# Two more gate chunks multiplied by seven in a four-layer transformer kernel, one of their joins inside the triangular solve, and a first input in longer runs

## The reference, cut to what matters

```
h = h + 0.5 * swiglu(rms_norm(h, ffn1_norm), ffn1_w_in, ffn1_w_out)
u = rms_norm(h, mix_norm)
z_s, xbc, dt, qkv, z_d, b, a, gate_s, gate_d = split(u @ w_in)
y_s = mamba2_branch(z_s, xbc, dt, ...)            # state space
y_d = deltanet_branch(qkv, z_d, b, a, ...)        # gated delta rule
merged = sigmoid(gate_s) * (y_s @ ssm_w_branch) + sigmoid(gate_d) * (y_d @ dn_w_branch)
h = h + merged @ w_out
h = h + 0.5 * swiglu(rms_norm(h, ffn2_norm), ffn2_w_in, ffn2_w_out)
```

## Time and profile before

| | |
|---|---|
| median of 3 runs (lowest, highest) | 3190.79 us (3189.23, 3192.85) |
| the profiled execution's own time | 3191.32 us |
| its span, first to last instruction | 3189.5 us |
| PE busy / DVE busy / ACT busy / POOL busy | 3175.9 / 2379.4 / 665.3 / 281.8 us |
| granted TensorE clock, mean | 0.999 |
| share of PE in the chain that ended last | 99% |

### The profile page before, as it was taken

One profiled execution on the slowest core, in us unless ns is written; L12 is line 12 of the kernel. 1 busy time (PEld: TensorE's weight loads), 2 busy tenths in 40 slices (PEclk: granted clock), 3 DMA queues, 4 the chain that ended last, 5 costly groups with the idle time before them and its releaser, 6 DMA issues.

```text
span 3189.5 us, 59761 instructions
## 1 busy us (share of the span) xinstructions
PE 3175.9 (100%) x25296; PEld 3035.7 (95%) x25296; DVE 2379.4 (75%) x4672; ACT 665.3 (21%) x1633; POOL 281.8 (9%) x329
## 2 busy tenths in 40 slices
PE   9999999999999999999999999999999999999998
PEld 8999999999999999999999999879999999889998
DVE  6657887476666578874867898877786888876885
ACT  1113433211111134332211111211211111212211
POOL 0202000001102020000011000300021000300031
PEclk9999999999999999999999999999999999999999
DMA  5444444345445444443544444344445444343453
GB/s 204 171 156 140 143 147 151 119 159 172 171 160 172 159 136 143 150 151 120 184 172 165 167 168 165 130 149 146 150 168 172 164 168 171 119 159 133 159 173 133
DMA packets 89787, 497.52 MB, mean 156 GB/s; under 512 B 25104, under 2 KB 29616, under 8 KB 30640
## 3 DMA queue, kind: packets, MB, share of 16 engines
q1 hardware_dynamic: 70752, 489.45, 44.5%
q10 hardware_dynamic: 18768, 4.25, 0.7%
HBM read 491.55 MB, written 2.11 MB: 155 GB/s over the span
## 4 chain that ended last, share of the span: by engine, by line
PE 99%; DMA 1%; DVE 0%; ACTq 0%; SPq 0%; ACT 0%; issue 0%; DVEq 0%
PE bank L358 92%; PE bank L2109 1%; PE bank L2921 0%; PE bank L2163 0%; PE bank L2865 0%; PE bank L2902 0%; PE bank L2088 0%; DMA ring<-w 0%; DMA hT<-hT_d 0%; PE bank L531 0%; PE bank L2866 0%; PE bank L2040 0%; PE bank L2110 0%; PE bank L2126 0%; PE bank L2048 0%; PE bank L2846 0%
## 5 line engine op out<-in xcount | busy, mean ns | idle before, releaser
L358 PE MATMUL bank<-arena 128*128 128x128 f32 x9480 | 1122.4, 275 | 0.0
L358 PEld LDWEIGHTS bank<-arena 128*128 128x128 f32 x9480 | 1089.9, 192 | 0.2 <-DVE arena L1087 0.2
L358 PE MATMUL bank<-arena,ring 128*128 128x128 f32 (+1 forms) x6408 | 1000.4, 309 | 2.5 <-ACT arena L891 2.1
L358 PEld LDWEIGHTS bank<-arena,ring 128*128 128x128 f32 x6408 | 907.0, 191 | 59.2 <-issue 2.9
L358 PE MATMUL bank<-xT,ring 128*128 128x128 f32 (+1 forms) x4816 | 666.4, 292 | 0.1
L358 PEld LDWEIGHTS bank<-xT,ring 128*128 128x128 f32 x4816 | 620.2, 192 | 21.8 <-issue 1.0
L1085 DVE TENSOR_TENSOR arena<-ring 128x1024 f32<-128x1024 f32 x355 | 435.4, 1226 | 104.0 <-PE bank L358 93.5
L1032 ACT ACTIVATE arena<-bank 128x128 f32<-128x128 f32 x323 | 89.0, 275 | 990.7 <-PE bank L358 985.2
L1140 DVE TENSOR_TENSOR arena<-arena,bank 128x256 f32<-128x256 f32 x323 | 136.0, 421 | 202.3 <-PE bank L358 189.5
L1137 DVE TENSOR_TENSOR arena<-arena,bank 128x256 f32<-128x256 f32 x323 | 134.4, 416 | 191.7 <-ACT arena L1032 191.6
L358 PE MATMUL bank<-xT,arena 128*128 128x128 f32 x2072 | 276.6, 275 | 0.6 <-DVE arena L1073 0.6
(11 more groups left out here) (331 smaller groups left out, 2131.2 us busy)
## 6 DMA issues: line engine op xcount, KB each, us to landing
ring<-w SPq DMA_DIRECT2D x460, 1024.0 KB, 4.9
hT<-hT_d ACTq DMA_DIRECT2D x4, 256.0 KB, 6.7
ring<-w SPq DMA_DIRECT2D x4, 256.0 KB, 6.6
ring<-w SPq DMA_DIRECT2D x2, 512.0 KB, 4.6
arena<-blocks_d ACTq DMA_DIRECT2D x4, 256.0 KB, 6.0
arena<-base_d ACTq DMA_DIRECT2D x16, 64.0 KB, 3.9
arena<-memT_d SPq DMA_DIRECT2D x1, 1024.0 KB, 8.1
outT<-hT SPq DMA_DIRECT2D x4, 256.0 KB, 2.5
```

Of the source, the lines that this page charges most:

```text
L358: ins = self.e.matmul(out, lhsT, rhs, start=start, stop=stop)
```

## The change

1. `gate_d` 0 and `gate_s` 3 are multiplied by seven. They become the first two of five `gd_7` chunks, and `branch_s` 1 moves between them, in the chunks' order and in PE's: `branch_s` 0, `gate_s` 3, `branch_s` 1, `gate_d` 0, `branch_s` 2 to 5. They use token sums that exist already.
2. DVE makes the first one's weight sums in place of the memset, behind a wait for ACT's tanh of the third `gate_s` chunk, and joins it before kk times the decays. The memset and the second one's sums stand ahead of the solve. `branch_s` 1 is gated behind step 10 of the solve and the second chunk is joined behind step 15. The third chunk's weight sums stand ahead of the transpose of the solved blocks, not behind it.
3. ACT copies the two parts, takes the squares of q behind the second chunk's product, and the two tanhs from SBUF behind the joins.
4. The first chunk and the input lie in HBM so that each of the eight first transfers is 128 runs of 2 KB; the first opening reads its weight tiles in the new order.
5. ACT gets a table load ahead of its wait for the gain vector.

```diff
 def opening(...):
-            i = m * KD + k
+            i = 2 * k + m if n == 0 and not again else m * KD + k
...
 def bulk_jobs():
-        spec += many(L, "branch_s", 1, "dve") + many(L, "gate_d", 1, "act") + many(L, "gate_s", 1, "act", 3)
-        spec += many(L, "branch_s", 5, "dve", 1) + both(L, "gd_7", 3) + many(L, "branch_s", 2, "dve", 6)
+        gates = both(L, "gd_7", 5)
+        spec += many(L, "branch_s", 1, "dve") + gates[0:2] + many(L, "branch_s", 1, "dve", 1) + gates[2:4]
+        spec += many(L, "branch_s", 4, "dve", 2) + gates[4:] + many(L, "branch_s", 2, "dve", 6)
...
-    multiply_fast(_L, "gd_7", _L * CHUNKS1 + 80, 3, 3, True)
+    multiply_fast(_L, "gd_7", _L * CHUNKS1 + 73, (0, 2, 7, 8, 9), 5, True)
...
 def first_act(...):
     else:
+        e.preload_act_table_set(LN_EXP)
         e.wait_ge(sems.gain_loaded, 16)
     norm_by_act(a, m, 3 * L, row("ffn1_norm", KD))
...
+    part_by_act(a, m.seven_g0, L, "gd_7", 0)          # behind the decays' exponentials
...
+    part_by_act(a, m.seven_g1, L, "gd_7", 1)          # behind the blocks' DMA issues
+    e.wait_ge(sems.bulk_done, BULK.filled(L, "gd_7", (1, 1)))
     for i in range(4):
         e.activation(m.q_sq[:, i], m.qkv[:, 2 * i:2 * i + 2, :], ACT.Square, scale=P * EPS ** 0.5).then_inc(sems.squares_ready, 1)
         seen.up("squares_ready")
     e.preload_act_table_set(EXP_TANH)
-    gate(0)
-    e.wait_ge(sems.bulk_done, BULK.filled(L, "gate_s", 3))
-    e.activation(m.gate_s[:, 6:8, :], ..., ACT.Tanh, scale=0.5).then_inc(sems.bulk_read_act, 1)
+    late_gate(0)
+    late_gate(1)
     e.wait_ge(sems.base_solved, upto(L, "base_solved", 1))
...
 def first_dve(...):
     e.wait_ge(sems.normed, seen["normed"])
-    e.memset(m.inv_t, 0.0)
+    e.wait_ge(sems.gates_ready, upto(L, "gates_ready", 7))
+    weights_by_dve(v, m.seven_g, ring, FAST_FROM[L, "gd_7"])
...
+    join(v, m.seven_g0, L, "gd_7", 0, in_place=True, to=m.gate_s[:, 6:8, :])      # ahead of kk times the decays
...
     turned, x, part, x_t = m.base
+    e.memset(m.inv_t, 0.0)
+    weights_by_dve(v, m.seven_g1, ring, FAST_FROM[L, "gd_7"] + 1)
...
     for j in range(BASE - 1):
...
+        if j == 10:
+            branch_s(1)
+        if j == 15:
+            e.wait_ge(sems.bulk_done, BULK.filled(L, "gd_7", (1, 1)))
+            join(v, m.seven_g1, L, "gd_7", 1, in_place=True, to=m.gate_d[:, 0:2, :])
...
-    branch_s(1)
     for i in range(4, 8):
         kv_rows(i)
...
+    e.wait_ge(sems.base_stored, 32 * (L + 1))
+    weights_by_dve(v, m.seven_g, ring, FAST_FROM[L, "gd_7"] + 2)
     e.wait_ge(sems.base_loaded, 16 * BLOCKS * (L + 1))
     e.transpose(...).then_inc(sems.diag_turned, 1)
-    e.wait_ge(sems.base_stored, 32 * (L + 1))
-    weights_by_dve(v, m.seven_g, ring, FAST_FROM[L, "gd_7"])
...
 def first_pe(...):
-    t.product((L, "gate_d", 0), xT)
+    t.by_seven(L, "gd_7", (0,), m.seven_g0)
...
-    t.product((L, "gate_s", 3), xT)
-    for i in range(6):
+    for i in range(2):
+        beside()
+    t.by_seven(L, "gd_7", (1,), m.seven_g1)
+    for i in range(4):
         beside()
...
 def program(...):                                    # SP
-                    two = slice(2 * i, 2 * i + 2)
-                    e.dma_start(by_row(ring[:, 0, :])[:, :, two, :], by_row(w1[0])[:, :, two, :]).then_inc(sems.rows_loaded[i], 16)
+                    four = slice(4 * i * P, 4 * i * P + 4 * P)
+                    e.dma_start(ring[:, 0, four], w1[0][:, four]).then_inc(sems.rows_loaded[i], 16)
...                                                   # ACT
-                    e.dma_start(hT[:, two, :], hT_d.rearrange("(k p) n -> p k n", p=P)[:, two, :]).then_inc(sems.h_loaded[i], 16)
+                    e.dma_start(hT[:, two, :], hT_d.rearrange("p (k n) -> p k n", n=S)[:, two, :]).then_inc(sems.h_loaded[i], 16)
```

More of the change, by code:

```diff
@@ L843, in __init__ @@
         self.seven_g.part = self.gate_d[:, 6:8, P:S]
+        self.seven_g0 = Seven(arena, 0, 0, 0)
+        self.seven_g0.s, self.seven_g0.tx = self.seven_g.s, self.seven_x.tx
+        self.seven_g0.part = self.merged[:, 6:8, 0:P]
+        self.seven_g1 = Seven(arena, 48 * S, 0, 0)
+        self.seven_g1.tx, self.seven_g1.part = self.seven_x.tx, self.seven_g0.part
         self.seven_d = Seven(arena, 24 * S, 16 * S, 48 * S)
@@ L1439, in first_act, with late_gate @@
     e.wait_ge(sems.act_step, seen["act_step"])
+    def late_gate(i):
+        e.wait_ge(sems.bulk_read_dve, BULK.read(L, "gd_7", (i, 1)))
+        x = m.gate_d[:, 2 * i - 2:2 * i, :] if i else m.gate_s[:, 6:8, :]
+        e.activation(x, x, ACT.Tanh, scale=0.5).then_inc(sems.gates_ready, 1)
+        seen.up("gates_ready")
     for i in range(4):
@@ L1457, in first_act @@
     block = lambda x, b: units(x)[b * BASE:(b + 1) * BASE, :, b * BASE:(b + 1) * BASE]
[L1459 to L1462, removed]
     e.wait_ge(sems.beta_stored, 16 * (L + 1))
@@ L1489, in first_act @@
         e.dma_start(block(m.inv_t, b), by_unit(m.base_d)[:, b].rearrange("u i j -> i u j")).then_inc(sems.diag_loaded, 16)
[L1491 to L1495, removed]
     def negated(name, i, dst, rows, n):
@@ L1518, in first_act @@
         if name == "wt":
-            part_by_act(a, m.seven_g, L, "gd_7", 1)
+            part_by_act(a, m.seven_g, L, "gd_7", 3)
         if name == "state":
-            late_gate(1)
-    part_by_act(a, m.seven_g, L, "gd_7", 2)
+            late_gate(3)
+    part_by_act(a, m.seven_g, L, "gd_7", 4)
     for i in range(4):
@@ L1528, in first_act @@
         squares(m.sq_d[:, i, :], m.qkv[:, 2 * i:2 * i + 2, :])
-    late_gate(2)
+    late_gate(4)
     e.preload_act_table_set(LN_EXP)
@@ L1824, in branch_s @@
         if i == 6:
-            e.wait_ge(sems.bulk_read_act, BULK.read(L, "gate_s", 3))
+            e.wait_ge(sems.gates_ready, upto(L, "gates_ready", 9))
         stt(m.merged[:, i, :], m.gate_s[:, i, :], 1.0, b[:, 0:S], ALU.add, ALU.mult).then_inc(sems.bulk_read_dve, 1)
@@ L1916, in first_dve @@
     branch_s(5)
-    weights_by_dve(v, m.seven_g, ring, FAST_FROM[L, "gd_7"] + 1)
+    weights_by_dve(v, m.seven_g, ring, FAST_FROM[L, "gd_7"] + 3)
     for i in range(2):
@@ L1922, in first_dve @@
            beta[HALF_P:P, some].unsqueeze(2).to_broadcast([HALF_P, 8, HALF_P]), ALU.mult).then_inc(sems.chain_read_dve, 1)
-    for i in range(3):
-        join(v, m.seven_g, L, "gd_7", i, in_place=True, to=m.gate_d[:, 2 * i + 2:2 * i + 4, :])
-        if i == 0:
-            weights_by_dve(v, m.seven_g, ring, FAST_FROM[L, "gd_7"] + 2)
+    for i in range(2, 5):
+        join(v, m.seven_g, L, "gd_7", i, in_place=True, to=m.gate_d[:, 2 * i - 2:2 * i, :])
+        if i == 2:
+            weights_by_dve(v, m.seven_g, ring, FAST_FROM[L, "gd_7"] + 4)
     for i in range(4):
@@ L2177, in first_pe @@
     where = by_sums(xT, m.seven_g.tx)
-    quarters = iter([(i, at) for i in range(3) for at in range(0, GROUPS, 2)])
+    quarters = iter([(i, at) for i in range(2, 5) for at in range(0, GROUPS, 2)])
     open_banks = {}
@@ L3219 @@
     second = [pack_second(a, l) for l in range(DEPTH)]
+    rows = first[0][0][0]
+    rows[:] = rows.reshape(P, 2, KD, P).transpose(0, 2, 1, 3).reshape(P, SLOT).copy()
     arrays = {
-        "hT_d": a["x"][0].T, "memT_d": a["mem_2"][0].T, "pos_d": on_all(a["positions_2"].astype(np.int32)),
+        "hT_d": a["x"][0].T.reshape(KD, P, S).transpose(1, 0, 2).reshape(P, KD * S), "memT_d": a["mem_2"][0].T, "pos_d": on_all(a["positions_2"].astype(np.int32)),
         "p1": np.stack([p for _, p in first]), "w1": np.concatenate([w for w, _ in first]),
```

15 lines of the change are left out of this document (6 added, 9 removed).

## The result

The changed kernel takes 3195.49 us (median of 22 runs, 3191.66 to 3197.22), the kernel before in the same jobs 3190.27 (22 runs, 3188.93 to 3194.59): a ratio of 1.0014, interval 1.0007 to 1.0020. It is 5.2 us slower; the forecast was 3.4 us faster. The profiled execution took 3193.19 us, its span 3191.4.

A forecast was written before the change was run, and what follows sets the result against it. PE, busy for 3175.9 of 3189.5 us, was taken as the bound. The terms -2.64 (chunks), +0.4 (spreads) and -1.2 (start) sum to -3.44 us, so a median of 3187.4 us; range 3184.6 to 3191.8, chance 0.87.

The forecast's parts named there:

- 0.66 us for each chunk by seven: Gate chunks on PE: 6.25 us by seven against 6.91 plain; four chunks in two layers give -2.64 us.
- 0.2 us a layer at the spreads: PE's fourth spread before the solve waits for DVE's later copy of beta: 0.2 us a layer, bounds 0 and 0.9.
- DVE's added work ahead of the transpose: Solve's tail: join 1.51 and sums 2.58 us move the transpose from 561.81 to 565.73, no PE stall.
- The base load ... moves only by the join's 1.51 us, to 563.3: Solve's tail: the load that also releases the transpose comes at 563.3, covered by the weight sums.
- Line 2199's stall: PE's first product needing the transpose: taken as 0, bounded at 0 and 1.0 us a layer.
- Rival (c): Solve's tail becomes the bound through PE's wait at line 2199; at 4 us late, 3194.0 us; chance 0.08.
- The first product still starts near 7.1: Start: line 887 repeats its table load, so the load ahead costs nothing, at most 0.4 us, which is absorbed.
- The repeated table load: Start: the first norm loads its table again at line 887; if skipped, 0.9 us more could be had.
- The term of -1.2 us: Start: 2 KB input runs bring the last landing 1.2 us earlier; bounds 0 and -2.2 us.
- Rival (a): Start: run length doesn't matter, chunk 1 still asked for at 11.5, start unchanged; 3188.6 us; chance 0.15.
- Both signs that the prediction named for its failure: A PE wait for the transpose of over a microsecond, or chunk 1 issued after 11, would make the forecast wrong.

The follow-up runs named there:

- e18: e12 with 10 warm-up products on ones instead of 8: 3187.20 us.
- e19: The kernel of e12 run once more, unchanged: 3188.53 us.
- e12: Changed kernel with 1 KB runs again, one table load, and SyncE waiting for base stores before chunk 80, base loads before chunk 81: 3188.13 us.

## Why the prediction was wrong

- *0.66 us for each chunk by seven:* right. A replaced chunk takes 6.25 us (513.25 to 519.50), and the stretch without waits is 1.10 us shorter against 1.12.
- *0.2 us a layer at the spreads:* right. They take 1.08 us (512.17 to 513.25) against 0.87.
- *DVE's added work ahead of the transpose:* right. The sums end at 567.03; the forecast for the transpose, 565.73, moved by the start's 2.04 us, is 567.77.
- *"The base load ... moves only by the join's 1.51 us, to 563.3":* this step failed. The stores did move by that order (556.37 against 553.23, less 2.04: 1.1 us), and the weight chunk was asked for 1.1 us earlier, as the prediction had it too (554.43 to 553.3); but the two were not set against each other, and together they put the stores behind the chunk which they had led by 1.83 us. The base load released the transpose at 570.35, less 2.04 some 5 us behind the forecast. Line 2199's stall was bounded at 1.0 us a layer from the spread between two layers of one order; the other order cost 1.85 here (65.96 less 64.11). SP's queue was looked at for when its chunk would be there, not for what it would do to the stores. Rival (c) had the place and mechanism, at a smaller price than its 3.3 us a layer: 2 x 1.85 = 3.7 us.
- *"The first product still starts near 7.1":* this step failed too, and it decides. The repeated table load was foreseen, and the last input did come earlier (chunk 1 asked for at 11.01, 0.5 us earlier and not 1.2). But half as many runs also take SP less time to issue, which was not counted; so the gain vector was asked for level with a 256 KB transfer, TensorE idled for 3.8 us, and the opening began at the half level, which no term of the sum had. The term of -1.2 us, bounded at 0 and -2.2, measures +2.04 in the profile.
- *Rival (a) and the rule behind it (the Trainium skill, "DMA: Bandwidth & Descriptors", Specifications):* 2 KB runs moved at 401 GB/s from 7 to 9 us (360 before) but at 189 from 5 to 7 (225 before). That is 1.18 MB against 1.17 over the four microseconds: nearly alike, as the rule has it, and not what the term of -1.2 us needed. But the longer runs acted through the time to issue, of which neither spoke, and chunk 1 was asked for at 11.01 and not still at 11.5.
- *Sum:* -2.64 + 0.4 + 3.7 + 2.04 = +3.5 us, against 5.2 measured. The 1.7 us between lie within what falls of the clock do to single executions (1.6 to 3.2 us each), but their share isn't shown. (The range's upper end, 3191.8, was set 0.2 us under the prediction's own bound of 3192.0; nothing hangs on that.) Both signs that the prediction named for its failure came: a wait of PE for the transpose of over a microsecond, and chunk 1 issued after 11.

## What to carry to other kernels

Before moving a small transfer that something waits for, or shortening the issue of a large one, list what every queue asks for within a microsecond of it: one place behind a large transfer brought the gain vector 2.4 us later at the start and made the stores take 3.3 us longer in the stage. A speed-up moves the requests that hang on the faster engine, too. Let the large one wait for the small one's semaphore where it has the time. Where a late input leaves TensorE idle at the start, price the clock of what follows as well as the wait, or give it work up to the first product.

## What was not expected of the hardware

- The landing of a 4 KB transfer went from 3.1 to 5.5 us, and of a 128 KB store from 2.5 to 5.8, by nothing but a large transfer asked for at the same time or 0.37 us earlier on another queue.
- With twelve more warm-up products, which feed nothing, the changed kernel's median was 5.7 us lower, 1.75 us of which its trace shows at the start. Four more in the kernel before gave 1.4, within the noise.
- TensorE's granted clock fell to half for 3.4 or 6.8 us in the middle of a kernel in which it had no gap (e18 at 574.7 us), and in some executions of a kernel only (e19, not e12).
